# Interleaving each block's product with rounded weights and its product with the weights' rest on TensorE

## The chip, the cores and the metric

The kernel runs on one core of one Trainium2 chip. The time is device microseconds of one execution. All times in the tables are medians of several executions of the same program.

## What is computed

Two transformer blocks are applied to one sequence of 256 tokens with 1024 features, everything in 32-bit floats. Cut to the matrix products that matter here, the reference is:

```python
# first block
x = x + 0.5 * swiglu(rms_norm(x, ffn1_norm), w_gate, w_up, w_down)      # gu0, down0
u = rms_norm(x, mix_norm) @ w_in                                        # w_in
x = x + concat([fourier_mixer(u), gqa_attention(u)]) @ w_out            # w_out
x = x + 0.5 * swiglu(rms_norm(x, ffn2_norm), w_gate, w_up, w_down)      # gu1, down1
x = rms_norm(x, final_norm)
# second block, layers 0 and 1
x = x + short_conv_mixer(h, conv_w_in, conv_w, conv_w_out)              # conv_in, conv_out
x = x + moba_attention(h, ...)                                          # moba, moba_o
x = x + mem_cross_attention(h, mem, w_q, w_kv, w_o)                     # mem0, mem_o0; mem1, mem_o1
x = x + (silu(g) * u) @ w_down      # g, u = split(h @ w_gu)            # gu2, down2; gu3, down3
```

The names behind the `#` are the phases of the kernel.

## The kernel before

**How a product is made.** TensorE multiplies 32-bit numbers fast only in a rounded form (fp32r). So each weight matrix W and each operand A is split in two rounded parts, W = Wh + Wl and A = Ah + Al, and three of the four products are added up: Wh Ah, Wh Al and Wl Ah. Ah and Al of the 256 tokens lie side by side in SBUF, so one matmul with Wh (helper `with_hi`, L418) streams 512 columns and writes Wh Ah into columns 0 to 255 of a PSUM bank and Wh Al into columns 256 to 511. A second matmul with Wl (L462 in square tiles, `with_rest`, L422, in the down phases) streams the 256 columns of Ah and adds to columns 256 to 511 of the same bank. Here these are called the 512-column and the 256-column products. Each has a 128x128 weight load of its own.

**Tiles.** All weights form one stream of 205 tiles (list `STREAM`) of 16 blocks of 128x128. Tile t lies in slot t % 3. SyncE loads it (L354; L365 to L369 for the down phases), ScalarE rounds it (L916, semaphore `weight_hi`), VectorE subtracts to get the rest (L1271, semaphore `weight_lo`), and TensorE uses both. TensorE counts `tile_done` behind its last product; on that ScalarE overwrites the slot's rounded half with tile t+3 and copies the second column half of the result out of PSUM (`rest`, L928). VectorE adds the two halves (L1376), scales them (L1400), makes the next tile's rest but one (L1271) and finishes the nonlinear part (L1416, L1422).

**Order on TensorE.** A square tile (`square_tile`, L424; 8 row blocks k by 2 output blocks m) waits for `weight_hi`, runs its 16 products of 512 columns, waits for `weight_lo`, runs its 16 products of 256 columns. First tiles of a phase are cut into shorter pieces (`cuts`), since their operand arrives in pairs of row blocks. Tiles that share TensorE with attention come in pieces (`PIECES`, `ks`). `value_tile` (L493) does the same with the roles of weights and operand swapped, with both weight parts needed from the start. `down` (L604) runs 16 blocks of a tile in the same two runs in `run` (L612). The phases `w_in` and `moba` use another form (`narrow`), where all products have 256 columns.

The engines' own programs set the order; there is no scheduler. The queue of each engine runs in order and waits at semaphores.

Of the kernel before, what the change touches and what calls it, by code (L numbers as in the profile page):

```python
# [14 lines left out]
S = 256  # L15
D = 1024
KB = D // P
KP = KB // 2
NT = S // P
# [30 lines left out]
for _name, _n in STREAM:  # L50
# [22 lines left out]
    ("mem1", [B, C, A, B] + [A, B] * 3), ("mem_o1", [A, B, C, A]),  # L73
    ("gu3", [B, C, A] * 7 + [B]), ("down3", [C, A, DD, B]),
]


NARROW = ("w_in", "moba")
# [96 lines left out]
def program(nc, weights, x_t, mem_t, vectors, consts, fourier, fnet_w, positions, out_t):  # L175
    ctx = ExitStack()
    with ctx:
# [237 lines left out]
        def _(pe):  # L415
# [8 lines left out]
            def square_tile(t, out, a, ready=None, beside={}, lows=None, ks=(0, KB), ms=2, cuts=(), narrow=False, late=None):  # L424


                w = wt[t % RING]
                for k0, k1 in zip((ks[0], *cuts), (*cuts, ks[1])):
# [24 lines left out]
                    if rest_first:  # L453
                        continue
                    if lows is not None:
                        pe.wait_ge(*lows(k0))
                    elif k0 == 0:
                        pe.wait_ge(weight_lo, t + 1)
                    for k in range(k0, k1):
                        for m in range(ms):  # L460
                            home = out[:, m, 0:S] if narrow else out[:, m, S:2 * S]
                            mm = pe.matmul(home, w[:, 1, m * KB + k, :], a[:, k, 0, :], start=False, stop=k == KB - 1,  # L462
                                           skip_group_check=True)
                if late is not None and narrow:
# [28 lines left out]
            def value_tile(t, out, a, beside={}, ks=(0, KB), narrow=False):  # L493

                w = wt[t % RING][:].rearrange("p a (m k) c -> p a m k c", m=2)
                if narrow:
                    narrow_values(t, out, a, w, beside, ks)
                    return
                o = [out[:, n, :].rearrange("p (a m c) -> p a m c", a=2, m=2) for n in range(NT)]
                tok = [slice(n * P, (n + 1) * P) for n in range(NT)]  # L500
                if ks[0] == 0:
                    pe.wait_ge(weight_lo, t + 1)
                for k in range(*ks):
                    if k in beside:
# [79 lines left out]
            def gate_up(n, name):  # L584
# [3 lines left out]
                for j in range(FF):  # L588
                    ready = operand(name) if j == 0 else None
                    in_parts = n == 0 and j < RING  # L590
                    lows = None
                    if in_parts and j == 0:
                        ready = lambda k: ([(first_split, 1)] if k == 0 else [(split_done, 1)] if k == 1 else operand(name)(k)) + (
                            [] if k % 2 else [(first_hi, 1)] if k == 0 else [(start_hi, k // 2)] if k < KB - 2 else [(weight_hi, 1)])
                        lows = lambda k: (start_lo, k // 2 + 1) if k < KB - 2 else (weight_lo, 1)
                    elif in_parts:
                        ready = lambda k: {0: [(start_hi, KP - 2 + j)], KB // 2: [(weight_hi, j + 1)]}.get(k, [])
                        lows = lambda k: (weight_lo, j + 1) if k else (start_lo, KP - 1 + j)
                    square_tile(t0 + j, banks_for(phase, j), xn, ready=ready, lows=lows,
                                beside={**norm(name, n == 0).get(j, {}), **tables.get(j, {})}, ms=1 if j == FF - 1 and n < 2 else 2,  # L600
                                cuts=((2, 4, 6) if j == 0 else (4,)) if in_parts else (4, 6) if j == 0 else (),
                                late=KP * OPERAND[name] if j == 0 and n else None)

            def down(n_ffn, norm_name, beside={}):  # L604
# [4 lines left out]

                    return [(8 * half0 + 4 * n, k) for n, k in enumerate(ks)]  # L610

                def run(i, rows, d, ms, fresh=False, final=None):  # L612

                    w = wt[(t0 + i) % RING]
                    blocks = [(at + m, k, m, bank[:, 2 * PAIR[name, 2 * d + m // 2] + m % 2, :])
                              for at, k in rows for m in ms]
                    for at, k, m, out in blocks:
                        if k == FF - 1 and name in SHORT:
                            pe.matmul(out[:, 0:S], w[:, 0, at, :], h[:, k, 0, :], start=False, stop=False, skip_group_check=True)
                        else:  # L620
                            with_hi(out, w[:, 0, at, :], h[:, k], k == 0)
                    if fresh:
                        pe.wait_ge(weight_lo, t0 + i + 1)
                    for at, k, m, out in blocks:
                        mm = with_rest(out, w[:, 1, at, :], h[:, k], k == final)
                        if k == final and (d, m) in ((0, 1), (0, 3), (1, 1), (1, 2)):
                            mm.then_inc(acc_done, 1)
                    return mm

                def final_run(i):  # L630
# [17 lines left out]
                for i in range(FF // 2):  # L648
# [5 lines left out]
                    if i <= FF // 4:  # L654
                        pe.wait_ge(h_split, FF * n_ffn + min(4 * i + 4, FF))
                    if i < FF // 4:
                        mm = run(i, rows_at(0, range(4 * i, 4 * i + 4)), 0, range(4), True)
# [19 lines left out]
            def residual(name, ready, b0=0, b1=KP, ks=None):  # L677

                for b in range(b0, b1):
                    k0, k1 = ks or (BEGUN.get(name, {}).get(b, 0), KB)  # L680
                    square_tile(FIRST[name] + b, banks_for(name, b, k0 == 0), h, ready=ready if b < 2 else None, ks=(k0, k1),
                                cuts=(6,) if b == 0 and k0 < 6 < k1 else ())

            def part(kind, j, ks=(0, KB), **more):
                what = PARTS[kind][j][0]
# [5 lines left out]
                if what == "v":  # L691
                    value_tile(t, out, src, ks=ks, beside=more.get("beside", {}), narrow=kind in NARROW)
                else:
                    square_tile(t, out, src, ks=ks, narrow=kind in NARROW, **more)

            def pieces(kind, n, i, ready):
                for j, k0, k1 in PIECES[kind][n][i]:
# [174 lines left out]
            for j in range(COUNT["conv_in"]):  # L872
                square_tile(FIRST["conv_in"] + j, banks_for("conv_in", j), xn, ready=operand("mix0") if j == 0 else None,
                            cuts=() if j else (4, 6), late=None if j else KP * OPERAND["mix0"],
                            beside={1: {5: both_sums}, 2: {1: lambda: spread_factor("mix0")}, 3: {1: lambda: spread_column(col_1, SPREAD_AT["mix0 first"], 0)}}.get(j, {}))
            for ks in ((0, 6), (6, KB)):
                for b in range(2):
# [1118 lines left out]
```

## Time and profile before

| | before |
|---|---|
| median of 3 executions | 1240.01 us |
| lowest, highest | 1239.48, 1240.45 us |
| span of the profiled execution, first to last instruction | 1237.7 us |
| TensorE busy | 1229.1 us (99%) |
| TensorE weight loads busy | 1095.2 us (88%) |
| VectorE busy | 928.1 us (75%) |
| ScalarE busy | 658.7 us (53%) |
| bytes moved | 221.74 MB |

The profiled execution is shown by its span; the median of the timed ones lies 2.3 us above it. Matmuls overlap in the profile (a product's recorded time includes its way through the array), so how fast they follow each other is read from the starts of rows, not from the duration of one. In a row of the timeline the first number is the start and the second the time from the start of the first to the end of the last instruction of a merged group; `PE` are matmuls and `PEld` the weight loads.

### The profile page before, as it was taken

Reading aid. Unit: us, or ns where it says so; the run is one execution under the profiler, and the core shown is the slowest. Engines: PE = TensorE matmul, PEld = TensorE weight load, DVE = VectorE, ACT = ScalarE, POOL = GpSimd, SP = SyncE. Lnnn points to the kernel's source line nnn. Section 1 sums busy time; section 2 is a strip of 40 time slices with the busy share of each in tenths; the row PEclk is TensorE's granted clock in tenths of the full one; section 3 lists DMA queues with packets and bytes.
Section 4 is the critical chain, followed back from the end, with each engine's and each line's share of the span. In section 5 each row is a group of like instructions: output and inputs, shape, how many; then the busy total and the mean of one; then the engine's idle time right before and its main releaser. Section 6 shows DMA issues by size and latency. Waiting matters only on the chain.

```text
span 1237.7 us, 18082 instructions
## 1 busy us (share of the span) xinstructions
PE 1229.1 (99%) x7432; PEld 1095.2 (88%) x7432; DVE 928.1 (75%) x1292; ACT 658.7 (53%) x872; POOL 31.1 (3%) x23
## 2 busy tenths in 40 slices
PE   9999999999999999999999999999999999999998
PEld 8888889978888888888888888889998888888887
DVE  7887866878777858988568777669968657877744
ACT  6655544456555444546546555445555445555632
POOL 0000000000000000440000000000000000000000
PEclk9999999999999999999999999999999999999999
DMA  9565664235555663556346555644445533555560
GB/s 329 187 213 177 224 209 164 75 137 172 187 186 188 214 216 131 186 188 211 130 138 233 188 190 186 222 170 152 156 142 182 187 136 137 204 200 177 198 209 34
DMA packets 51426, 221.74 MB, mean 179 GB/s; under 512 B 4464, under 2 KB 5776, under 8 KB 30864
## 3 DMA queue, kind: packets, MB, share of 16 engines
q1 hardware_dynamic: 51056, 220.25, 51.7%
q8 instruction: 59, 0.97, 0.3%
q10 hardware_dynamic: 288, 0.33, 0.1%
q14 instruction: 23, 0.19, 0.0%
HBM read 219.52 MB, written 1.05 MB: 178 GB/s over the span
## 4 chain that ended last, share of the span: by engine, by line
PE 92%; DVE 5%; issue 1%; DMA 1%; ACT 0%; SPq 0%; DVEq 0%; ACTq 0%
PE bank L418 48%; PE bank L462 21%; PE bank L422 7%; PE bank L449 5%; PE bank L507 2%; DVE wt L1271 2%; PE bank L761 2%; PE bank L789 2%; PE bank L484 1%; PE bank L510 1%; PE bank L489 1%; DMA raw<-weights 1%; PE bank L777 0%; PE bank L544 0%; DVE xn L1280 0%
## 5 line engine op out<-in xcount | busy, mean ns | idle before, releaser
L1271 DVE TENSOR_TENSOR wt<-raw,wt 128x2048 fp32r<-128x2048 f32 x202 | 464.1, 2299 | 67.8 <-ACT wt L916 67.4
L916 ACT ACTIVATE wt<-raw 128x2048 fp32r<-128x2048 f32 x202 | 386.0, 1911 | 119.7 <-PE bank L422 89.8
L418 PE MATMUL bank<-xn,wt 128*128 128x512 f32 x1712 | 416.3, 393 | 1.4 <-DVE scratch L1376 0.7
L418 PEld LDWEIGHTS bank<-xn,wt 128*128 128x128 f32 x1712 | 313.0, 188 | 63.0 <-DVE xn L1280 1.1
L418 PE MATMUL bank<-h,wt 128*128 128x512 f32 x1004 | 246.1, 392 | 0.0
L462 PEld LDWEIGHTS bank<-xn,wt 128*128 128x128 f32 x1824 | 234.3, 191 | 9.7 <-DVE wt L1271 0.8
L462 PE MATMUL bank<-xn,wt 128*128 128x256 f32 x1824 | 238.2, 283 | 0.2 <-DVE wt L1271 0.2
L418 PEld LDWEIGHTS bank<-h,wt 128*128 128x128 f32 x1004 | 182.5, 188 | 34.1 <-issue 0.4
L1376 DVE TENSOR_TENSOR scratch<-bank,rest 128x512 f32<-128x512 f32 x98 | 67.6, 690 | 86.9 <-ACT rest L928 86.8
L999 ACT ACTIVATE h<-scratch 128x256 fp32r<-128x256 f32 x88 | 36.8, 418 | 158.7 <-DVE scratch L1416 158.7
L928 ACT ACTIVATE rest<-bank 128x512 f32<-128x512 f32 x114 | 67.6, 593 | 65.9 <-PE bank L462 64.4
L422 PEld LDWEIGHTS bank<-h,wt 128*128 128x128 f32 x700 | 91.8, 191 | 4.6
L422 PE MATMUL bank<-h,wt 128*128 128x256 f32 x700 | 93.5, 282 | 0.0
L1400 DVE TENSOR_TENSOR scratch<-scratch,r_x 128x512 f32<-128x512 f32 x86 | 59.5, 692 | 2.9
L955 ACT ACTIVATE xn<-x,vec 128x256 fp32r<-128x256 f32 x62 | 28.1, 501 | 55.6 <-DVE x L1286 55.6
L462 PEld LDWEIGHTS bank<-h,wt 128*128 128x128 f32 x384 | 50.9, 191 | 2.8
L462 PE MATMUL bank<-h,wt 128*128 128x256 f32 x384 | 52.0, 282 | 0.0
L1285 DVE SCALAR_TENSOR_TENSOR x<-bank,x 128x512 f32<-128x512 f32 (+1 forms) x39 | 24.9, 637 | 30.6 <-PE bank L462 18.1
L1416 DVE TENSOR_TENSOR scratch<-scratch 128x256 f32<-128x256 f32 x88 | 36.7, 417 | 4.7 <-ACT scratch L997 4.7
L997 ACT ACTIVATE scratch<-scratch 128x256 f32<-128x256 f32 x88 | 35.7, 406 | 6.0 <-DVE scratch L1400 5.0
L449 PE MATMUL bank<-xn,wt 128*128 128x256 f32 x280 | 38.1, 288 | 0.0
L1422 DVE TENSOR_TENSOR h<-scratch,h 128x256 fp32r<-128x256 f32 x88 | 36.7, 417 | 0.6 <-ACT h L999 0.2
(227 smaller groups left out, 972.3 us busy)
## 6 DMA issues: line engine op xcount, KB each, us to landing
raw<-weights SPq DMA_DIRECT2D x158, 1024.0 KB, 4.9
raw<-weights SPq DMA_DIRECT2D x88, 512.0 KB, 4.9
raw<-weights SPq DMA_DIRECT2D x8, 256.0 KB, 4.5
k_t<-mem_t SPq DMA_DIRECT2D x2, 1024.0 KB, 8.1
raw<-weights SPq DMA_DIRECT2D x8, 128.0 KB, 4.1
out_t<-work SPq DMA_DIRECT2D x4, 256.0 KB, 2.3
x<-x_t SPq DMA_DIRECT2D x3, 256.0 KB, 5.3
v_s<-fourier SPq DMA_DIRECT2D x2, 256.0 KB, 5.3
```

The lines of the kernel that those rows point to most:

```text
L418: return pe.matmul(out, hi, a.rearrange("p a s -> p (a s)"), start=first, stop=False, skip_group_check=True)
L422: return pe.matmul(out[:, S:2 * S], lo, a[:, 0, :], start=False, stop=last, skip_group_check=True)
L449: pe.matmul(out[:, m, 0:S], w[:, 0, m * KB + k, :], a[:, k, i, :], start=k == i == 0, stop=False, skip_group_check=True)
L462: mm = pe.matmul(home, w[:, 1, m * KB + k, :], a[:, k, 0, :], start=False, stop=k == KB - 1, skip_group_check=True)
L916: act.activation(wt[t % RING][:, 0], raw[t % RING][:], ACT.Copy).then_inc(weight_hi, 1)
L928: act.activation(rest_s[i % 3][:], src, ACT.Copy).then_inc(rest_copied, 1)
L999: act.activation(h[:, j, 0, :], gate, ACT.Copy).then_inc(h_rounded, 1)
L1271: dve.tensor_tensor(wt[t % RING][:, 1], raw[t % RING][:], wt[t % RING][:, 0].bitcast(F32), ALU.subtract).then_inc(weight_lo, 1)
L1376: e = dve.tensor_tensor(dst, pair_banks(name, j)[:, :, 0:S], rest_s[i % 3][:], ALU.add)
L1400: dve.tensor_tensor(gu_s[j % 3], gu_s[j % 3], both(r_x[:]), ALU.mult).then_inc(drained, 1)
L1416: dve.tensor_tensor(gate, gate, up, ALU.mult).then_inc(whole, 1)
L1422: dve.tensor_tensor(h[rows, j, i, :], gu_s[j % 3][rows, 0, :], h[rows, j, 0, :].bitcast(F32), ALU.subtract).then_inc(h_split, 1)
```

## The change

Each 256-column product is issued right behind the 512-column product of a block, for the same block or for one that lies `lag` row blocks back. With lag 0 the two alternate strictly: 512, 256, 512, 256. With lag L a tile starts with 2L products of 512 columns, goes on in alternation, and ends with 2L products of 256 columns (beside the last pair's own). A table `LAG` gives the lag by phase and tile; other whole tiles have 0, and tiles that begin as a piece have 2. The wait for `weight_lo` moves from behind all 512-column products of a tile to behind the first 2L. In `run` of `down` the lag counts blocks, and only the tiles 0 and 1 of each down phase have one (10 blocks). `value_tile` alternates its two kinds as well (two and two). What stays as it was: the first tiles of phases with `cuts`, the narrow phases, the last products of the program (`final_run`), all counts of instructions, and the programs of the other four engines.

```diff
+LAG = {**{(f"gu{n}", j): (4 if n == 0 else {1: 5}.get(j, 3)) for n in range(4) for j in range(14 if n == 0 else 7)},
+       **{(f"down{n}", i): 5 for n in range(4) for i in range(2)},
+       **{("conv_in", j): 8 if j < 6 else 6 if j < 9 else 4 for j in range(12)},
+       ("w_out", 2): 8, ("w_out", 3): 5, ("conv_out", 0): 4, ("conv_out", 1): 4, ("conv_out", 2): 6, ("conv_out", 3): 4,
+       ("mem_o0", 2): 6, ("mem_o0", 3): 4, ("mem_o1", 2): 6, ("mem_o1", 3): 4,
+       **{("moba_o", b): 2 for b in range(4)},
+       ("mem0", 1): 7, ("mem0", 2): 3, ("mem1", 1): 5, ("mem1", 2): 2}
+
+def lag_of(name, j, k0, k1):
+    return min(LAG.get((name, j), 2 if k1 < KB else 0), k1 - k0) if k0 == 0 else 0
...
                 w = wt[t % RING]
+                if lag is not None:
+                    if ks[0] == 0:
+                        pe.wait_ge(weight_hi, t + 1)
+                    for k in range(ks[0], ks[1] + lag):
...
+                        if ks[0] == 0 and k == lag:
+                            pe.wait_ge(weight_lo, t + 1)
+                        for m in range(ms):
+                            if k < ks[1]:
+                                with_hi(out[:, m, :], w[:, 0, m * KB + k, :], a[:, k], k == 0)
+                            if k - lag >= ks[0]:
+                                mm = with_rest(out[:, m, :], w[:, 1, m * KB + k - lag, :], a[:, k - lag], k - lag == KB - 1)
+                    if ks[1] == KB:
+                        mm.then_inc(tile_done, 1)
+                    return
...
-                for k in range(*ks):
-                    for n in range(NT):
                         mm = pe.matmul(o[n][:, 1], a[:, k, 1, tok[n]], w[:, 0, :, k, :], start=False, stop=k == KB - 1,
...
-                    if fresh:
-                        pe.wait_ge(weight_lo, t0 + i + 1)
-                    for at, k, m, out in blocks:
-                        mm = with_rest(out, w[:, 1, at, :], h[:, k], k == final)
...
+                    for n in range(len(blocks) + lag):
+                        if n < len(blocks):
+                            at, k, m, out = blocks[n]
...
+                                with_hi(out, w[:, 0, at, :], h[:, k], k == 0)
+                        if n == lag and fresh:
+                            pe.wait_ge(weight_lo, t0 + i + 1)
+                        if n >= lag:
+                            at, k, m, out = blocks[n - lag]
+                            mm = with_rest(out, w[:, 1, at, :], h[:, k], k == final)
```

TensorE's order in phase gu3, tiles 11 and 12 (slots wt0 and wt1), in the kernel before:

```order
L418 MATMUL bank<-xn,wt0 128x512 [waits weight_hi,taken]
L418 MATMUL bank<-xn,wt0 128x512 x15
L462 MATMUL bank<-xn,wt0 128x256 [waits weight_lo]
L462 MATMUL bank<-xn,wt0 128x256 x15
L418 MATMUL bank<-xn,wt1 128x512 [waits weight_hi,taken]
```

The same place after the change, from the end of tile 11 into tile 12 (lag 0):

```order
L431 MATMUL bank<-xn,wt0 128x512
L435 MATMUL bank<-xn,wt0 128x256
L431 MATMUL bank<-xn,wt1 128x512 [waits weight_lo,weight_hi,taken]
L435 MATMUL bank<-xn,wt1 128x256
L431 MATMUL bank<-xn,wt1 128x512
L435 MATMUL bank<-xn,wt1 128x256
L431 MATMUL bank<-xn,wt1 128x512
L435 MATMUL bank<-xn,wt1 128x256
```

L431 and L435 are `with_hi` and `with_rest` in the changed file. The wait for the rest of the weights has moved from the seventeenth product of a tile to its first.

TensorE's order in phase gu0, tile 4 (slot wt1), in the kernel before:

```order
L418 MATMUL bank<-xn,wt1 128x512 [waits weight_hi,taken]
L418 MATMUL bank<-xn,wt1 128x512 x15
L462 MATMUL bank<-xn,wt1 128x256 [waits weight_lo]
L462 MATMUL bank<-xn,wt1 128x256 x15
```

And after, where the lag of this tile and its neighbours is 4 (what follows the rows shown is more of the same alternation, and then nine products of 256 columns in a row):

```order
L431 MATMUL bank<-xn,wt1 128x512 [waits weight_hi,taken]
L431 MATMUL bank<-xn,wt1 128x512 x7
L431 MATMUL bank<-xn,wt1 128x512 [waits weight_lo]
L435 MATMUL bank<-xn,wt1 128x256
L431 MATMUL bank<-xn,wt1 128x512
L435 MATMUL bank<-xn,wt1 128x256
```

The wait for the rest has moved from behind 16 products to behind 8. In the whole program a 256-column product follows a 512-column one directly at 240 places before and at 2,223 after, and 2,120 single 256-column products stand behind a single 512-column one, where before there was none. All of it is on TensorE; the order of the other engines' instructions is the same.

## Rows read from the trace of the kernel before

**Rows 1.** The page: span, busy time by engine, granted clock, chain by engine.

```profile
span 1237.7 us, 18082 instructions
...
PE 1229.1 (99%) x7432; PEld 1095.2 (88%) x7432; DVE 928.1 (75%) x1292; ACT 658.7 (53%) x872; POOL 31.1 (3%) x23
...
PEclk9999999999999999999999999999999999999999
...
PE 92%; DVE 5%; issue 1%; DMA 1%; ACT 0%; SPq 0%; DVEq 0%; ACTq 0%
```

**Rows 2.** The waits of TensorE: for whom, us in total, times, longest.

```profile
PE bank L418 <- DVE scratch L1376: 0.7, 1, 0.7
...
PE bank L462 <- DVE wt L1271: 0.2, 1, 0.2
```

**Rows 3.** Timeline of TensorE in gu3: start, us, engine, line, operation, count.

```profile
1100.12 3.82 PE L418 MATMUL bank<-xn,wt 128*128 128x512 f32 x16
1103.77 2.08 PE L462 MATMUL bank<-xn,wt 128*128 128x256 f32 x16
1105.68 3.82 PE L418 MATMUL bank<-xn,wt 128*128 128x512 f32 x16
1109.34 2.08 PE L462 MATMUL bank<-xn,wt 128*128 128x256 f32 x16
1111.25 3.82 PE L418 MATMUL bank<-xn,wt 128*128 128x512 f32 x16
```

**Rows 4.** The timeline cut narrowly, to see each run's second product start.

```profile
1105.92 0.40 PE L418 MATMUL bank<-xn,wt 128*128 128x512 f32 x1
...
1103.88 0.40 PE L462 MATMUL bank<-xn,wt 128*128 128x256 f32 x2
```

**Rows 5.** Timeline of TensorE in w_out, where runs are two long.

```profile
279.74 0.63 PE L418 MATMUL bank<-h,wt 128*128 128x512 f32 x2
280.21 0.39 PE L462 MATMUL bank<-h,wt 128*128 128x256 f32 x2
280.44 0.63 PE L418 MATMUL bank<-h,wt 128*128 128x512 f32 x2
280.90 0.40 PE L462 MATMUL bank<-h,wt 128*128 128x256 f32 x2
281.13 0.63 PE L418 MATMUL bank<-h,wt 128*128 128x512 f32 x2
```

**Rows 6.** Timeline of TensorE at the end of down0: runs of three, one bank each.

```profile
189.60 0.86 PE L418 MATMUL bank<-h,wt 128*128 128x512 f32 x3
190.30 0.52 PE L422 MATMUL bank<-h,wt 128*128 128x256 f32 x3
190.66 0.86 PE L418 MATMUL bank<-h,wt 128*128 128x512 f32 x3
191.35 0.52 PE L422 MATMUL bank<-h,wt 128*128 128x256 f32 x3
191.71 3.71 PE L449 MATMUL bank<-xn,wt 128*128 128x256 f32 x28
```

**Rows 7.** Timeline of VectorE in gu3: the chain that ends with a weight rest.

```profile
1106.51 0.69 DVE L1376 TENSOR_TENSOR scratch<-bank,rest 128x512 f32<-128x512 f32 x1 [1.28 <-ACT rest L928]
1107.24 0.69 DVE L1400 TENSOR_TENSOR scratch<-scratch,r_x 128x512 f32<-128x512 f32 x1
1107.85 2.28 DVE L1271 TENSOR_TENSOR wt<-raw,wt 128x2048 fp32r<-128x2048 f32 x1
```

**Rows 8.** Timeline in gu0, tiles 5 and 6: TensorE's starts and VectorE's rests.

```profile
36.97 3.82 PE L418 MATMUL bank<-xn,wt 128*128 128x512 f32 x16
37.00 2.29 DVE L1271 TENSOR_TENSOR wt<-raw,wt 128x2048 fp32r<-128x2048 f32 x1
...
42.45 2.28 DVE L1271 TENSOR_TENSOR wt<-raw,wt 128x2048 fp32r<-128x2048 f32 x1
...
42.54 3.82 PE L418 MATMUL bank<-xn,wt 128*128 128x512 f32 x16
```

**Rows 9.** Timeline in conv_in, tiles 9 and 11: VectorE's rests, TensorE's starts.

```profile
525.47 2.28 DVE L1271 TENSOR_TENSOR wt<-raw,wt 128x2048 fp32r<-128x2048 f32 x1
...
525.97 3.82 PE L418 MATMUL bank<-xn,wt 128*128 128x512 f32 x16
...
536.75 2.27 DVE L1271 TENSOR_TENSOR wt<-raw,wt 128x2048 fp32r<-128x2048 f32 x1
...
537.10 3.82 PE L418 MATMUL bank<-xn,wt 128*128 128x512 f32 x16
```

More of the change, by code:

```diff
@@ L422, in with_rest, with square_tile @@
                 return pe.matmul(out[:, S:2 * S], lo, a[:, 0, :], start=False, stop=last, skip_group_check=True)
-            def square_tile(t, out, a, ready=None, beside={}, lows=None, ks=(0, KB), ms=2, cuts=(), narrow=False, late=None):
+            def square_tile(t, out, a, ready=None, beside={}, lows=None, ks=(0, KB), ms=2, cuts=(), narrow=False, late=None, lag=None):
                 w = wt[t % RING]
+                if lag is not None:
+                    if ks[0] == 0:
+                        pe.wait_ge(weight_hi, t + 1)
+                    for k in range(ks[0], ks[1] + lag):
+                        if k < ks[1] and ready is not None:
+                            for s, value in ready(k):
+                                pe.wait_ge(s, value)
+                        if k < ks[1] and k in beside:
+                            beside[k]()
+                        if ks[0] == 0 and k == lag:
[8 more added lines that the diff above has]
+                    return
                 for k0, k1 in zip((ks[0], *cuts), (*cuts, ks[1])):
@@ L601, in gate_up @@
                                 cuts=((2, 4, 6) if j == 0 else (4,)) if in_parts else (4, 6) if j == 0 else (),
+                                lag=None if in_parts or j == 0 else lag_of(phase, j, 0, KB),
                                 late=KP * OPERAND[name] if j == 0 and n else None)
@@ L610, in rows_at, with run @@
                     return [(8 * half0 + 4 * n, k) for n, k in enumerate(ks)]
-                def run(i, rows, d, ms, fresh=False, final=None):
+                def run(i, rows, d, ms, fresh=False, final=None, lag=0):
                     w = wt[(t0 + i) % RING]
@@ L616, in run @@
                               for at, k in rows for m in ms]
-                    for at, k, m, out in blocks:
[L618 to L621, printed above, removed]
-                    if fresh:
-                        pe.wait_ge(weight_lo, t0 + i + 1)
-                    for at, k, m, out in blocks:
-                        mm = with_rest(out, w[:, 1, at, :], h[:, k], k == final)
-                        if k == final and (d, m) in ((0, 1), (0, 3), (1, 1), (1, 2)):
-                            mm.then_inc(acc_done, 1)
+                    for n in range(len(blocks) + lag):
+                        if n < len(blocks):
+                            at, k, m, out = blocks[n]
+                            if k == FF - 1 and name in SHORT:
+                                pe.matmul(out[:, 0:S], w[:, 0, at, :], h[:, k, 0, :], start=False, stop=False, skip_group_check=True)
+                            else:
+                                with_hi(out, w[:, 0, at, :], h[:, k], k == 0)
[4 more added lines that the diff above has]
+                            mm = with_rest(out, w[:, 1, at, :], h[:, k], k == final)
+                            if k == final and (d, m) in ((0, 1), (0, 3), (1, 1), (1, 2)):
+                                mm.then_inc(acc_done, 1)
                     return mm
@@ L656, in down @@
                     if i < FF // 4:
-                        mm = run(i, rows_at(0, range(4 * i, 4 * i + 4)), 0, range(4), True)
+                        mm = run(i, rows_at(0, range(4 * i, 4 * i + 4)), 0, range(4), True, lag=2 * LAG.get((name, i), 0))
                     elif i == FF // 4:
@@ L681, in residual @@
                     square_tile(FIRST[name] + b, banks_for(name, b, k0 == 0), h, ready=ready if b < 2 else None, ks=(k0, k1),
-                                cuts=(6,) if b == 0 and k0 < 6 < k1 else ())
+                                cuts=(6,) if b == 0 and k0 < 6 < k1 else (),
+                                lag=None if b == 0 and k0 < 6 < k1 else lag_of(name, b, k0, k1))
             def part(kind, j, ks=(0, KB), **more):
@@ L693, in part @@
                 else:
-                    square_tile(t, out, src, ks=ks, narrow=kind in NARROW, **more)
+                    square_tile(t, out, src, ks=ks, narrow=kind in NARROW,
+                                lag=None if kind in NARROW else lag_of(kind, j, *ks), **more)
             def pieces(kind, n, i, ready):
@@ L874, in _ @@
                             cuts=() if j else (4, 6), late=None if j else KP * OPERAND["mix0"],
+                            lag=lag_of("conv_in", j, 0, KB) if j else None,
                             beside={1: {5: both_sums}, 2: {1: lambda: spread_factor("mix0")}, 3: {1: lambda: spread_column(col_1, SPREAD_AT["mix0 first"], 0)}}.get(j, {}))
```

## The prediction

> **What bounds the kernel now.** I read the page first: TensorE is busy for 1229.1 of 1237.7 us, the chain that ended last runs over TensorE for 92% of the span, and the granted clock stands at nine tenths or more of full speed, the level of 2.4 GHz, in all 40 slices [rows 1]. Then the list of waits: the longest that TensorE stood still for another engine is 0.7 us, and for a weight rest it waited once, 0.2 us [rows 2]. So no wait is left whose removal could pay. What remains is how fast products follow each other. That is read from starts in the timeline, not from durations, because matmuls overlap. In gu3 the starts of three 512-column runs are 1100.12, 1105.68 and 1111.25 [rows 3]: two tiles of 16 + 16 products in 11.13 us, or 11.13 / 32 = 0.3478 us for one pair of a 512- and a 256-column product. Inside, 16 products of 512 take 1103.77 - 1100.12 = 3.65 us and 16 of 256 take 1105.68 - 1103.77 = 1.91 us, so 228 and 119 ns each. The column counts alone, at 2.4 GHz, are 213 and 107 ns, so each product, long or short, carries some 13 to 15 ns beyond its columns. That is the whole stake of this change: it takes away no product and no weight load, it only changes which product follows which.
>
> **The change, part by part: the pace.** The instruction order shows 2,120 single 256-column products that come to stand directly behind a single 512-column one. The price of such a pair in strict alternation is nowhere in this trace: the shortest runs are two long. It must be bounded from rows.
>
> Runs of two: the starts 279.74, 280.44 and 281.13 [rows 5] give 1.39 us for four pairs, 0.3475 us a pair. Runs of three, three products into one PSUM bank each: 189.60 to 191.71 [rows 6] is 2.11 us for six pairs, 0.3517 us. Runs of sixteen: 0.3478 us [rows 3]. The upper bound is that of the runs of three. It is not monotone: the blocks of three are dearer than both of the others, and those of two are as cheap as those of sixteen.
>
> The lower bound comes from the edges of long runs. The first 256-column product behind a 512-column run lasts 1103.88 - 1103.77 = 0.11 us to the next start [rows 3, 4], less than the 0.119 of its run. The first 512-column product behind a 256-column run lasts 1105.92 - 1105.68 = 0.24 us [rows 3, 4], while the other fifteen of a run have (3.65 - 0.24) / 15 = 0.227. If alternation kept the cheap edge and paid nothing for it, a pair would cost 0.11 + 0.227 = 0.337 us. If it paid both edges, 0.11 + 0.24 = 0.35 us. I take the runs of two, since they are the nearest thing to alternation that the trace has: 0.3475. Against the present 0.3478 that is 2,120 x -0.3 ns = -0.6 us. The ends of the range are 2,120 x -10.8 ns = -22.9 us and 2,120 x +3.9 ns = +8.3 us.
>
> That a 256-column product adds to the very bank that the product before it writes should cost nothing: in the runs of three with one bank each the step from the last 512 to the first 256 is part of 190.30 - 189.60 = 0.70 us for three [rows 6], 0.23 each, no gap among them. That holds for the lagged tiles too, since block m of both kinds goes to the same bank.
>
> A rule of the Trainium skill speaks against a gain here. Its page "TensorE: Matmul & The Clock Gate" (section "Step-by-step: what each phase is for") says that the next weights are loaded while the running matmul streams, and (section "LDWEIGHTS (loading the stationary operand)") that a load of 128 columns takes about 107 ns. By that each short product just covers the load of the next and each long one covers it twice over, and alternation leaves the number of loads under short products as it was, so its sum would be no change in pace. Its figures for the gap (section "Back-to-back issue gap": 518 and 262 cycles, 216 and 109 ns) would give 325 ns a pair in either order; the trace has 348, so the measured number stands.
>
> **The change, part by part: the wait for the weights' rest.** Before, 16 products of 512 columns (3.65 us) covered VectorE's subtraction at the start of a tile. Now 2L of them do, and none at lag 0. What stands behind the waiting instruction is the whole rest of the tile on TensorE, and behind that `tile_done`, for which ScalarE's copy and next rounding wait. So lateness would go into the end of the tile one to one. I compare for each kind of tile the end of the rest with the moment of the new wait.
>
> Steady tiles of gu1, gu2, gu3 (lag 0): the chain behind a finished tile is L1376, L1400, L1271, and ends at 1107.85 + 2.28 = 1110.13 [rows 7]; the tile that needs it starts at 1111.25 [rows 3]. It is 1.12 us early with no cover at all: free. It hangs on the end of a TensorE tile, so it moves with it, and would still be free with tiles shorter by a tenth.
>
> Gu0, tiles 5 to 9 (lag 4): tile 5 starts at 36.97 and its rest is ready at 37.00 + 2.29 = 39.29. The old wait came at 36.97 + 3.65 = 40.62, the new one after eight products at 36.97 + 8 x 0.228 = 38.79: late by 0.50 us. Tile 6 starts at 42.54, and with the shift of 0.50 its wait comes at 44.86, behind the rest at 42.45 + 2.28 = 44.73 [rows 8]. So this is paid once.
>
> Conv_in, where VectorE is busiest: tile 9 would wait at 525.97 + 1.82 = 527.79, its rest is there at 527.75; tile 11 at 537.10 + 1.82 = 538.92 with the rest at 539.02, late by 0.10 us [rows 9]. Each late wait also costs the weight load that can't be issued ahead, about one short interval of 0.11 us [rows 4]. Sum: 0.50 + 0.10 + 2 x 0.11 = +0.8 us. It is bounded below by 0 (the engines before it may shift a little, too) and above by about 3 us, if some six tiles of this kind lose 0.5 each as the one in gu0.
>
> Nothing else moves: all other queues (SyncE's loads wait for `weight_lo`, which VectorE gives at the same place of its program) have the same order, and the products at the end of the program keep theirs. Earlier `acc_done` marks in the down phases feed VectorE, which isn't on the path.
>
> **Sum.** -0.6 + 0.8 = +0.2 us. The profiled span of 1237.7 us lies 2.3 us below the median of the timed runs; I add the change to the median: 1240.0 + 0.2 = 1240.2 us.
>
> **The rivals.**
>
> A, faster: the short product's extra time belongs to a run of short ones, where one weight load treads on the heels of the next. Then alternation keeps the cheap edge of 0.11 us at all 2,120 places. For it: the first short product of each run is faster than the others [rows 3, 4]. Against it: the first long product behind a short run is slower by about as much (0.24 against 0.227), and runs of two show no gain. Full price: -22.9 + 0.8, 1217.9 us. Half of it: 1229.4 us.
>
> B, slower: changing from short to long costs the long ones something, as the dearer runs of three show. The number of such changes goes from 207 to 2,188 in the instruction order. Price at the pace of runs of three: +8.3 + 0.8, 1249.1 us. It decides from a pair of 0.3486 us on, where 2,120 x 0.8 ns + 0.8 us make 2.5 us. Against it: the runs of two.
>
> C, slower by waits: more tiles of gu0 and conv_in come late to their rests. Up to +3 us, 1243 us; it lies at the edge of what can be told from no change. If A holds, these waits grow, since VectorE there doesn't get faster.
>
> **How the numbers follow.** A measurement of this kernel can tell about 0.2%, 2.5 us, from no change. The forecast's own case, a pair between 0.3465 and 0.3486 us, gets 0.46. A gets 0.30: two thirds of it for up to half of its price, one third for more. B gets 0.20 and C 0.04. So faster by over 0.2%: 0.30; within 0.2%: 0.46; slower: 0.24. The range goes from 1228 us (half of A and a little more) to 1249 us (all of B but its tail); what is left out is the far part of A and the tail of B.
>
> **What would show it.** In the profile after, the distance of two tile starts in gu3 divided by 16 is the pair: 0.3475 us if I am right, 0.34 or less for A, 0.35 or more for B. The waits of TensorE should name L1271 with about 1 us in all, most of it near 38.8 us in gu0, and next to nothing in gu3. The weight loads should still be 7,432, and the granted clock unchanged. I am wrong in the main if the distance of gu3 tiles leaves 5.55 to 5.58 us, since 2,120 pairs multiply each nanosecond of it into 2.1 us.

## The result, and the profile after

The changed kernel takes 1249.09 us (four runs, 1248.88 to 1249.15), the kernel before 1239.93 us on the same chip (four runs, 1239.48 to 1240.45). The ratio is 1.0074, with a 95% interval of 1.0062 to 1.0086: slower by 9.2 us. The forecast said 1240.2 and no difference. The profiled executions show the same step: the span goes from 1237.7 us [rows 1] to 1247.3 us.

The page of the changed kernel: span, busy time by engine (share, instructions), the granted clock, and the chain that ended last, by engine.

```profile
span 1247.3 us, 18090 instructions
...
PE 1238.6 (99%) x7432; PEld 1092.5 (88%) x7432; DVE 928.7 (74%) x1292; ACT 659.4 (53%) x872; POOL 31.1 (2%) x23
...
PEclk9999999999999999999999999999999999999999
...
PE 91%; DVE 6%; ACT 1%; issue 1%; DMA 1%; SPq 0%; DVEq 0%; ACTq 0%
```

TensorE has the same 7,432 products and 7,432 weight loads as in [rows 1], the same clock, and 9.5 us more busy time. VectorE and ScalarE did the same work in the same time. So the kernel did not begin to wait for another engine; the products themselves follow each other more slowly. The waits of TensorE for what the change could touch (for whom, us in total, times, longest) confirm it:

```profile
PE bank L431 <- DVE scratch L1413: 0.8, 1, 0.8
...
PE bank L431 <- DVE wt L1308: 0.3, 1, 0.3
PE bank L435 <- DVE wt L1308: 0.2, 1, 0.2
```

The first is the wait that [rows 2] had too (0.7). The second is new and is the late weight rest of gu0; the third was there before. Together they explain well under 1 us of the 9.6. (`with_hi` is at line 431 now, `with_rest` at 435, the weight rest at 1308.)

The rest is in the distance of tiles. VectorE makes one weight rest per tile right behind the tile before, so its starts are a clean ruler. Three rests in gu3 of the changed kernel (start, duration):

```profile
1110.09 2.28 DVE L1308 TENSOR_TENSOR wt<-raw,wt 128x2048 fp32r<-128x2048 f32 x1
...
1115.74 2.29 DVE L1308 TENSOR_TENSOR wt<-raw,wt 128x2048 fp32r<-128x2048 f32 x1
...
1121.40 2.29 DVE L1308 TENSOR_TENSOR wt<-raw,wt 128x2048 fp32r<-128x2048 f32 x1
```

Two tiles in 11.31 us, where [rows 3] had 11.13. A pair now takes 11.31 / 32 = 0.3534 us, not 0.3478. But this is not the pace everywhere. The start times in two cuts of TensorE's timeline, the first from gu3 and the second from the late tiles of gu0, which run the very same order of instructions (one 512-column product, one 256-column product, lag 0):

```profile
1107.92 0.40 PE L431 MATMUL bank<-xn,wt 128*128 128x512 f32 x1
1108.15 0.28 PE L435 MATMUL bank<-xn,wt 128*128 128x256 f32 x1
1108.27 0.40 PE L431 MATMUL bank<-xn,wt 128*128 128x512 f32 x1
...
1108.63 0.40 PE L431 MATMUL bank<-xn,wt 128*128 128x512 f32 x1
...
1108.98 0.40 PE L431 MATMUL bank<-xn,wt 128*128 128x512 f32 x1
...
1110.04 0.40 PE L431 MATMUL bank<-xn,wt 128*128 128x512 f32 x1
```

```profile
120.06 0.39 PE L431 MATMUL bank<-xn,wt 128*128 128x512 f32 x1
...
120.41 0.39 PE L431 MATMUL bank<-xn,wt 128*128 128x512 f32 x1
...
120.76 0.39 PE L431 MATMUL bank<-xn,wt 128*128 128x512 f32 x1
...
122.14 0.39 PE L431 MATMUL bank<-xn,wt 128*128 128x512 f32 x1
```

In gu3 six pairs take 1110.04 - 1107.92 = 2.12 us, 0.3533 a pair, and the steps go 0.35, 0.36, 0.35: one pair in three is longer. In gu0 six pairs take 122.14 - 120.06 = 2.08 us, 0.3467 a pair, with even steps. I call these the **slow pace** and the **fast pace**. The same order of products has two prices, 6.7 ns apart, and each lasts for many tiles: all of gu1, gu2 and gu3 from tile 7 on run slow, the late tiles of gu0 run fast. Both can stand in one phase: in down1 the 52 pairs from 428.20 us on run slow, then come nine 256-column products in a row, and the 72 pairs from 447.53 us on run fast. Of all pairs in stretches of 20 or more, 1,160 ran slow and 216 fast. Both levels are above 0.320 us, which is 768 columns at 2.4 GHz, so the fast pace is 13.3 ns beyond the columns for each product, just what the long products in runs of sixteen have (0.227 us). Split by product (starts in the trace to the nanosecond, means over the 240 pairs of gu3), the slow pace is 236.7 ns for the long and 116.7 for the short one. The fast pace, in the late tiles of gu0, is 230.0 and 116.7. So in both the short product is cheaper than the 120 ns that it has within a run, and in both the long one is dearer than its 227; the two paces differ in the long product alone.

By phase, each counted from its first product to that of the next phase, changed kernel minus kernel before: gu0 +1.2, down0 +0.8, gu1 +1.5, down1 +0.3, gu2 +1.6, down2 +0.8, gu3 +1.5, down3 +0.8, the other ten phases together +1.4; sum +9.9. The span grew by 9.6, because the first product of gu0 starts 0.3 us earlier in this trace; 0.24 of gu0's 1.2 is that start and not the change. In gu3, 15 tiles at 5.653 us in place of 5.567 make 1.3 of the 1.5; the lagged tiles before them make the rest. Down1 lost less than the other down phases, since most of its strict pairs ran fast.

One thing said of the change above is not so in the code: `value_tile` alternates one by one, like the other tiles, and not two and two. In the diff both products stand in the same inner loop, and in mem0 the trace has 512, 256, 512, 256 columns from 569.11 us on.

### The profile page after: what moved, and what is told of

It is laid out like the page before. It is cut to its first block, busy times and chain, and to the rows that moved or that the text cites. A ratio compares the mean times of both kernels' runs of the same rounds, so it can differ in the third digit from the quotient of the medians.

```text
span 1247.3 us, 18090 instructions
## 1 busy us (share of the span) xinstructions
PE 1238.6 (99%) x7432; PEld 1092.5 (88%) x7432; DVE 928.7 (74%) x1292; ACT 659.4 (53%) x872; POOL 31.1 (2%) x23
## 4 chain that ended last, share of the span: by engine, by line
PE 91%; DVE 6%; ACT 1%; issue 1%; DMA 1%; SPq 0%; DVEq 0%; ACTq 0%
PE bank L431 48%; PE bank L435 24%; PE bank L481 5%; PE bank L494 3%; PE bank L539 2%; DVE wt L1308 2%; PE bank L825 2%; PE bank L797 2%; PE bank L516 1%; PE bank L540 1%; PE bank L521 1%; DMA raw<-weights 1%; PE bank L813 0%; PE bank L574 0%; DVE scratch L1413 0%
## 5 line engine op out<-in xcount | busy, mean ns | idle before, releaser
L431 PE MATMUL bank<-xn,wt 128*128 128x512 f32 x1712 | 553.6, 398 | 1.6 <-DVE scratch L1413 0.8
L435 PE MATMUL bank<-xn,wt 128*128 128x256 f32 x1632 | 392.8, 281 | 0.2 <-DVE wt L1308 0.2
L431 PEld LDWEIGHTS bank<-xn,wt 128*128 128x128 f32 x1712 | 317.1, 188 | 74.6 <-DVE wt L1308 1.1
L431 PE MATMUL bank<-h,wt 128*128 128x512 f32 x1004 | 328.9, 397 | 0.0
L435 PEld LDWEIGHTS bank<-xn,wt 128*128 128x128 f32 x1632 | 283.2, 189 | 5.4 <-DVE wt L1308 0.8
L435 PE MATMUL bank<-h,wt 128*128 128x256 f32 x1012 | 247.9, 281 | 0.0
L431 PEld LDWEIGHTS bank<-h,wt 128*128 128x128 f32 x1004 | 186.7, 188 | 42.7 <-issue 0.4
L435 PEld LDWEIGHTS bank<-h,wt 128*128 128x128 f32 x1012 | 177.8, 189 | 2.4
L539 PE MATMUL bank<-wt,mn 128*128 128x512 f32 x128 | 46.1, 402 | 0.0
L481 PE MATMUL bank<-xn,wt 128*128 128x256 f32 x280 | 38.1, 288 | 0.0
L540 PE MATMUL bank<-wt,mn 128*128 128x256 f32 x128 | 35.9, 280 | 0.0
```

The source lines that it names most:

```text
L431: return pe.matmul(out, hi, a.rearrange("p a s -> p (a s)"), start=first, stop=False, skip_group_check=True)
```

## The experiments

**First question: what sets the pace?** In front of the stretch in gu0 that is fast, the last lagged tile has lag 4; in front of those that are slow in gu1 to gu3 it has lag 3. A lag of L row blocks leaves 2L long products ahead, so 16 - 2L pairs, and then 2L short products behind. Theory (P in the expectations): the pace is a cycle that TensorE falls into, and where the tile before it is cut decides which. The rivals: the phase decides, by its other work (S: traffic of VectorE, ScalarE and the transfers), or every change between long and short has its price (C, the prediction's rival B).

**e1_residue**: the changed kernel with one more row block of lag in tile 6 of gu1 to gu3, and half a row block more in tile 1 of the down phases.

```
-LAG = {**{(f"gu{n}", j): (4 if n == 0 else {1: 5}.get(j, 3)) ...
-       **{(f"down{n}", i): 5 for n in range(4) for i in range(2)},
+LAG = {**{(f"gu{n}", j): (4 if n == 0 else {1: 5, 6: 4}.get(j, 3)) ...
+       **{(f"down{n}", i): (5, 5.5)[i] for n in range(4) for i in range(2)},
```

> The changed kernel with two numbers of the table of lags altered: tile 6 of gu1, gu2 and gu3 has lag 4 in place of 3 (8 alternating pairs in it, not 10), and tile 1 of each down phase 11 blocks in place of 10 (5 pairs, not 6). Theory P (phase): strict alternation has two paces, 0.3533 us a pair (three pairs in 1.06 us) and 0.3467 us (three in 1.04 us), and which of them a stretch gets is set by where the stretch before was cut: 2, 5, 8 or 11 pairs behind a long run of 512-column products lead to the fast one. Then tiles 7 to 21 of gu1 to gu3 take 5.547 us each, not 5.653, the down tiles behind tile 1 likewise: 45 x -0.106 - some 25 x -0.1, together about -7 us, 1242 us. Theory C (each change from 256 to 512 columns costs the long product something, whatever came before): the number of changes is the same but for 9, so 1249 us. Theory S (the place decides: other engines' traffic in SBUF and PSUM): gu1 to gu3 keep 5.653, 1249 us.

Measured: 1244.11 us (1244.03 to 1244.52), ratio to before 1.0034 (1.0021 to 1.0047), 5.0 us below the changed kernel. Its weight rests in gu3:

```profile
1095.39 2.28 DVE L1308 TENSOR_TENSOR wt<-raw,wt 128x2048 fp32r<-128x2048 f32 x1
1100.94 2.29 DVE L1308 TENSOR_TENSOR wt<-raw,wt 128x2048 fp32r<-128x2048 f32 x1
...
1123.12 2.28 DVE L1308 TENSOR_TENSOR wt<-raw,wt 128x2048 fp32r<-128x2048 f32 x1
```

Five tiles in 27.73 us, 5.546 each: fast. Tiles 7 to 21 have not one instruction in another order than in the changed kernel; only tile 6 in front of them differs, and the 232 pairs (gu1) or 240 pairs (gu2, gu3) behind it changed pace. The three phases lost their 1.5 or 1.6 us each and stand 0.02 to 0.09 below the kernel before. So the price isn't that of the alternation itself, nor of the place in the kernel. The down phases stayed as they were, against the expectation: that half of the rule was wrong.

**e2_lags**: the same tile 6 with lag 7 in gu1, 5 in gu2 and 6 in gu3.

```
-LAG = {**{(f"gu{n}", j): (4 if n == 0 else {1: 5}.get(j, 3)) ...
+LAG = {**{(f"gu{n}", j): (4 if n == 0 else {1: 5, 6: {1: 7, 2: 5, 3: 6}[n]}.get(j, 3)) ...
```

> The changed kernel with the lag of tile 6 set apart by phase: 7 in gu1 (2 alternating pairs), 5 in gu2 (6 pairs), 6 in gu3 (4 pairs). Theory P: only gu1 gets the fast pace behind it (remainder 2 by 3), tiles of 5.547 us; gu2 and gu3 keep 5.653. A rival within P, that a longer lag as such or a later wait gives the fast pace: all three are fast. Theories C and S: none is. Time: 1249.1 - 15 x 0.106 = 1247.5 us by P, 1244.3 by the rival, 1249.1 by C and S.

Measured, one run: 1249.14 us, all three phases slow (1.4 to 1.5 us above the kernel before, each); the one expected to be fast (gu1, lag 7) was slow as well. So a rule by the number of pairs alone is not enough. Read product by product (starts to the nanosecond), the short products behind the cut have a rhythm of their own, whose longest step is 124 ns against 117 to 121 for the others. In the tiles that led to the fast pace, the run of short ones was left behind that long step: it was 9 long there, and 15 in gu1 here. From this the next runs' rule: of runs behind eight pairs, those of 9 and of 14 short products (the last pair's own counted) give the fast pace, the others the slow one.

**Second question: does it hold without the rest of the change?** **e3_strict** is the kernel before, in its two separate runs everywhere, but with tiles 7 to 21 of gu1 to gu3 in strict alternation. **e4_strict_kick** is e3 with tile 6 at lag 4 in front of them.

```
 e3:  LAG = {(f"gu{n}", j): 0 for n in (1, 2, 3) for j in range(7, FF)}
 e4:  LAG = {(f"gu{n}", j): 4 if j == 6 else 0 for n in (1, 2, 3) for j in range(6, FF)}
 both (a tile not in the table keeps its two runs):
      return min(LAG.get((name, j), KB), k1 - k0)
```

> The kernel before (two runs in each tile) with one part of the change: tiles 7 to 21 of gu1, gu2 and gu3 alternate strictly (lag 0), all else in two runs as before. Theory P: entered from a long run of 256-column products the stretch is slow, 5.653 us a tile against 5.567, 45 x 0.086 = +3.9 us over the kernel before, 1243.8 us. Theory C: the same, +3.9 us. My forecast on record would have been a pair of 0.3475 us and no difference.

> As the run before it, and tile 6 of the three phases has lag 4 (8 alternating pairs in front of the strict stretch). Theory P: the fast pace, 5.547 us a tile against 5.567 of two runs: 45 x -0.020 + 3 x 0.038 = -0.8 us against the kernel before, 1239.2 us, and 4.7 us below the run before it. Theories C and S: 45 x 0.086 + 3 x 0.04, +4.0 us, 1243.9 us, the same as the run before it.

Measured: e3 1243.55 us (1243.15 to 1244.74), ratio 1.0032 (1.0021 to 1.0044); e4 1239.16 us (1238.90 to 1239.97), ratio 0.9997 (0.9988 to 1.0006). This is the cleanest pair of the study: one number in the table moves the time by 4.4 us. TensorE's timeline at the beginning of the alternation in gu3, first e3 and then e4 (start, duration, line, operation, count):

```profile
1080.22 3.82 PE L425 MATMUL bank<-xn,wt 128*128 128x512 f32 x16
1083.88 2.08 PE L429 MATMUL bank<-xn,wt 128*128 128x256 f32 x16
...
1086.14 0.40 PE L425 MATMUL bank<-xn,wt 128*128 128x512 f32 x1
...
1086.50 0.40 PE L425 MATMUL bank<-xn,wt 128*128 128x512 f32 x1
...
1088.26 0.40 PE L425 MATMUL bank<-xn,wt 128*128 128x512 f32 x1
```

```profile
1078.32 2.23 PE L425 MATMUL bank<-xn,wt 128*128 128x512 f32 x9
...
1082.85 1.25 PE L429 MATMUL bank<-xn,wt 128*128 128x256 f32 x9
1083.93 0.40 PE L425 MATMUL bank<-xn,wt 128*128 128x512 f32 x1
...
1084.63 0.39 PE L425 MATMUL bank<-xn,wt 128*128 128x512 f32 x1
...
1086.71 0.39 PE L425 MATMUL bank<-xn,wt 128*128 128x512 f32 x1
```

Six pairs take 1088.26 - 1086.14 = 2.12 us in e3 and 1086.71 - 1084.63 = 2.08 us in e4: 353.3 and 346.7 ns. In e3 each of the three phases is 1.3 us longer than before, in e4 0.2 to 0.3 us shorter. The first two pairs of e4's stretch take 351 and 352 ns; from the third on the fast pace is there, and it stays to the end of the phase. Both forecasts of theory P were met within 0.3 us.

**Third question: is it the surroundings?** **e5_quiet** is the kernel before with 13 stretches of products behind its end, when every other engine and all transfers are idle. The stretches are long runs, some pairs, short runs of different lengths, and then 24 or 48 strict pairs; some put the short products into other banks than the long ones.

```
 for _ in range(longs):  long_one()
 for _ in range(pairs):  long_one(); short_one()
 for _ in range(shorts): short_one()
 for _ in range(strict): long_one(); short_one(other)
```

> The kernel before, and behind its end, when all other engines and the DMA are done, 13 stretches of strict alternation on TensorE alone, each behind 16 long products (512 columns) that level out what came before, then n alternating pairs, then a run of short products (256 columns), then 48 or 24 strict pairs; and 12 times two long, two short. The time is longer by these stretches, some 200 us, and tells nothing. Theory P, which the traces so far make sharper: the fast pace of 0.3467 us a pair needs n = 2 by remainder 3 and a run of short ones of 9 (8 and the last of the pairs) or 14, for that run then has a rhythm of five (121, 120, 124, 118, 117 ns) and has to end behind the 124. So: n = 0, 16 short ones: slow, 0.3533; n = 8 with 8 more: fast; the same two where the strict short products go to other banks than the long ones: unchanged, slow and fast; straight behind the long run: slow; n = 6 and n = 7: slow; n = 8 with 9, 10, 11, 12, 14 more: slow, with 13 more: fast. Theory S (traffic of other engines): with all others idle there is one pace only, 0.3467, in every stretch. Theory B (a short product that adds to the bank just written pays): other banks give 0.3467 where the same bank gave 0.3533. Two and two: 0.348 to 0.349 us a pair.

Measured: all 13 stretches ran at the pace that was expected of them. A window of this part (busy time of each engine, with instructions; granted clock, DMA share, GB/s), and then the cuts of the timeline in which two of the stretches begin and end:

```profile
1300.00:1350.00 50.00, 50.00 (x284) 43.59 (x283) 0.00 (x0) 0.00 (x0) 0.00 (x0) 1.00 0.00 1
```

```profile
1260.70 0.40 PE L418 MATMUL bank<-xn,wt 128*128 128x512 f32 x1
...
1277.66 4.04 PE L418 MATMUL bank<-xn,wt 128*128 128x512 f32 x17
1284.00 1.25 PE L422 MATMUL bank<-xn,wt 128*128 128x256 f32 x9
1285.09 0.40 PE L418 MATMUL bank<-xn,wt 128*128 128x512 f32 x1
...
1301.73 3.83 PE L418 MATMUL bank<-xn,wt 128*128 128x512 f32 x16
```

Behind 16 long and 16 short products, 48 pairs take 1277.66 - 1260.70 = 16.96 us, 353.3 ns each. Behind eight pairs and 9 short products, 48 pairs take 1301.73 - 1285.09 = 16.64 us, 346.7 ns each. With nothing else running on the core the two paces are the same as inside the kernel, as closely as these cuts can be read (0.2 ns a pair), so traffic and contention aren't what makes them two. With the short products in other banks the means were 353.4 and 346.9: the bank has no part either. Behind eight pairs, short runs of 10, 11, 12, 13 and 15 gave 352.7 to 353.3, and the run of 14 gave 347.1:

```profile
1470.95 1.85 PE L422 MATMUL bank<-xn,wt 128*128 128x256 f32 x14
...
1472.64 0.40 PE L418 MATMUL bank<-xn,wt 128*128 128x512 f32 x1
...
1480.97 4.06 PE L418 MATMUL bank<-xn,wt 128*128 128x512 f32 x17
```

(24 pairs in 8.33 us). Behind six or seven pairs a run of 9 gave 353.4 and 353.3. The end of this part held runs of two, as those of [rows 5]: 348.3 ns a pair.

**Fourth question: the late weight rest.** **e6_wait** is the changed kernel with lag 8, that is two separate runs, in tile 5 of gu0.

```
-... (4 if n == 0 else {1: 5}.get(j, 3)) ...
+... ((8 if j == 5 else 4) if n == 0 else {1: 5}.get(j, 3)) ...
```

> The changed kernel with tile 5 of gu0 in two runs (lag 8): its wait for the weights' rest stands behind 16 products again. In the trace of the changed kernel the start of tile 6 lies 0.60 us further behind the kernel before than the start of tile 5. If that is the late rest, it falls to about 0.0 and tile 7 pays at most 0.1; the phase of later stretches is not touched, since tiles 6 to 13 keep their lag: about -0.5 us in all, 1248.6 us. If it is pace, it stays.

Measured, one run: 1248.91 us. First the wait in the changed kernel, then the same place in e6, one tile later:

```profile
37.13 1.99 PE L431 MATMUL bank<-xn,wt 128*128 128x512 f32 x8
39.42 0.50 PE L431 MATMUL bank<-xn,wt 128*128 128x512 f32 x1 [0.30 <-DVE wt L1308]
39.76 0.28 PE L435 MATMUL bank<-xn,wt 128*128 128x256 f32 x1
```

```profile
37.29 3.81 PE L431 MATMUL bank<-xn,wt 128*128 128x512 f32 x16
40.94 2.08 PE L435 MATMUL bank<-xn,wt 128*128 128x256 f32 x16
42.85 2.62 PE L431 MATMUL bank<-xn,wt 128*128 128x512 f32 x9
45.31 0.28 PE L435 MATMUL bank<-xn,wt 128*128 128x256 f32 x1
```

In the changed kernel the eight long products would end at 37.13 + 8 x 0.228 = 38.95; the next starts at 39.42, 0.47 us late, and the step to its short product is 0.34 in place of 0.23 us. That is 0.58 us, and the tile is 0.60 us longer than before. In e6 it is gone there, but the next tile's nine long products and their gap take 45.31 - 42.85 = 2.46 us, where the same nine in the changed kernel's later tiles take 2.06: the wait was moved on by a tile and cost 0.40 us there, against the expectation of at most 0.1. VectorE is behind TensorE at that point of gu0, and in both kernels the first tile with half of the cover paid for it. The time, 0.2 us below the changed kernel's, fits the two numbers but couldn't show them by itself.

**Last: does the fast pace beat the kernel before?** **e7_fast** keeps the two separate runs, and in gu0 to gu3 and the down phases places one tile with eight pairs and then strict alternation.

```
 KICK = (13, 6, 6, 6)
 LAG = {(f"gu{n}", j): 4 if j == KICK[n] else 0 for n in range(4) for j in range(KICK[n], FF)}
 ... (down phases) lag=(16, 8, 0, 0, 0)[i]
```

> The kernel before with strict alternation only where the rest of the weights is early without cover, and each such stretch entered at the fast pace: tile 13 of gu0, tile 6 of gu1 to gu3 and tile 1 of each down phase have lag 4 (8 pairs, run of 9 short ones), the tiles behind them to the end of the phase lag 0; everything else in two runs. Theory P: gu0 8 tiles, gu1 to gu3 45 tiles and the down phases some 32, each 5.547 in place of 5.567 us, and 8 entry tiles at +0.04: 85 x -0.020 + 8 x 0.04 = -1.4 us, 1238.3 us. Theory C: 85 x 0.086 + 0.3, +7.6 us, 1247 us.

Measured: 1239.49 us (1238.99 to 1240.57, 11 runs) against 1239.80 (14 runs), ratio 0.9998 (0.9989 to 1.0008): no difference that can be told, 1.2 us above the expectation. By the trace six of its eight stretches were fast and gained 0.06 to 0.27 us each; down0 and the first part of down1 ran slow and lost 0.67 and 0.24. In down0 the tile with the eight pairs itself ran otherwise than in the later phases:

```profile
136.08 0.50 PE L571 MATMUL bank<-weigh,work 128*128 128x1 f32 x4
136.44 2.33 PE L426 MATMUL bank<-h,wt 128*128 128x512 f32 x9
138.61 0.28 PE L430 MATMUL bank<-h,wt 128*128 128x256 f32 x1
...
139.42 0.39 PE L426 MATMUL bank<-h,wt 128*128 128x512 f32 x1
...
140.11 0.39 PE L426 MATMUL bank<-h,wt 128*128 128x512 f32 x1
```

Four products of one column stand just ahead of it, and its pairs then ran in steps of 0.35 and 0.34 us, 0.69 us for two, where in the later phases they have the steps of the slow pace. The nine short products behind them don't end with a step of 124 ns, and the pace that followed was slow. That the one-column products are the cause isn't shown. Down1 speaks against them as the whole of it: no one-column product stands ahead of its tile, yet its eight pairs (from 421.36 us on) ran at the fast pace, and behind the same nine short ones the 52 pairs were slow. So the number of pairs and of short products doesn't settle the pace by itself; the steps in which the pairs run differ too, and what sets those is open.

## Why the prediction was wrong

**The step that failed is the price of a pair.** The working took 0.3475 us from the runs of two [rows 5] as the nearest thing to alternation, and made 2,120 x -0.3 ns = -0.6 us of it. The runs measured 0.3533 us in most stretches and 0.3467 us in a few. Over the whole kernel the phases show 9.9 us more; less 0.2 for the earlier start and 0.7 for the late rests (0.6 in gu0, 0.1 in conv_in) this is 9.0 / 2,120 = 4.2 ns a pair over the old 0.3478, so 0.3520 on average. The term was -0.6 and is +9.0. The forecast's own sign of being wrong was a distance of gu3 tiles outside 5.55 to 5.58 us; it is 5.653. Single stretches lie even above the upper bound of 0.3517 that I took from the runs of three [rows 6], and the fast ones are far above the lower bound of 0.337.

**What was wrong behind it** is the assumption that strict alternation has one price, for which short runs are a nearer and nearer stand-in. It has two, 2% apart, and TensorE stays in the one it enters. The rows hinted at this: blocks of three were dearer than both those of two and those of sixteen, which I wrote down as "not monotone" and then resolved by nearness. A price that isn't monotone in the length of the runs can't be carried to length one by nearness; it called for the wide chance on the slower side. The working also held the better term and passed it over: "if it paid both edges, 0.11 + 0.24 = 0.35 us". By it the term is 2,120 x +2.2 ns = +4.7 us. The slow pace pays about both edges: a short product of 0.117 us and a long one of 0.237.

**Rival A's premise fell.** The short product does keep a part of its cheap edge in alternation, 0.117 us in the mean against 0.120 in a run, but never without a dearer long one, 0.230 or 0.237 against 0.227. The cheap pair of 340 ns comes once, as the first of a lagged tile behind long products; the second has 350 already. In the fast pace a pair costs the columns and 13.3 ns for each product, as the long products in long runs do. What the short runs of the kernel before lose against that is 1.2 ns a pair. So at the best steady pace that any run showed there were 2,120 x 1.2 ns = 2.5 us to win, about what a measurement can just tell, and at the slow one 2,120 x 5.5 ns = 11.7 us to lose.

**Rival B had the time, and half of the mechanism.** It forecast 1249.1 us by a price that the long product pays for each change from short to long. A long product behind a short one does take longer, by 10 ns at the slow pace and by 3 at the fast one. But that is no fixed price: e1 has as many such changes as the changed kernel but for some ten in 2,188, e4 has some twenty more than e3, and they take 5.0 and 4.4 us less. That the sum agrees to the tenth of a microsecond is luck. B took 0.3517 us, close to the mean of 0.3520, from two pairs of blocks of three, read to 0.01 us [rows 6]. All four such pairs of blocks at the end of down0 in the kernel before, from 187.50 to 191.71 us, give 4.21 / 12 = 0.3508, and B would have said 1247.2.

**The waits were right.** The list of waits named the weight rest in gu0, at the tile and within 0.1 us of the size forecast (0.60 against 0.50 + 0.11). The steady tiles of gu1 to gu3 wait for nothing, as the chain of [rows 7] said. "Paid once" was right too; e6 shows that it is paid once even when the tile is spared. Conv_in is +0.3 us in all. Of it the late rests make 0.1, half of the forecast: the first pair takes 0.42 us in tile 8 (526.94 us) and 0.36 in tile 11, in place of 0.34. Rival C's 3 us didn't come.

**A rule weighed in the prediction.** The sum from the loads of weights was no change in pace, since the number of loads under short products is kept. The runs at hand decide otherwise: the pace changed by -1.2 or +5.5 ns a pair with the same loads. The Trainium skill's page "TensorE: Matmul & The Clock Gate" (section "Step-by-step: what each phase is for") has the next weights loaded under the running matmul. The trace agrees: in the changed kernel loads are busy for 1092.5 us and products for 1238.6 of the same 1247.3. But it doesn't tell the pace to a percent.

**What stays open** is what inside TensorE makes the two cycles. Shown by e5 to have no part in there being two: other engines, transfers, the bank, waits and the clock (1.00 for both); the number of products and loads is the same too. A wait or another product in between can still decide which of the two follows. That it is the phase between loading weights and streaming columns is a guess; no run here tells it from another one. The rule by the length of the last short run (9 or 14 behind eight pairs) foretold all 13 stretches of e5, but it missed where the tile before was entered otherwise (down0 and down1 in e7). In the changed kernel nine short products in a row stand ahead of 72 pairs in both down0 and down1, and the pairs are slow in the first and fast in the second. So the rule describes this order and is no law.

## What to carry to other kernels

When TensorE is the bound and a change only reorders its products, price the new order in its steady state, and don't infer it from short runs of another shape: here six pairs in one cycle take 2.12 us and in another 2.08 us, and 2,000 of them make 13 us. Read the distance of tiles in each phase after such a change, since the same code can run at two paces; if it does, try the cut of the tile in front before giving the order up. And compute first what a perfect order could win (columns plus the fixed part seen in the best rows): here that was 2.5 us of 1240, a fifth of what the slow pace can cost.

## What the runs showed that was not expected

Products of 512 and 256 columns in strict alternation, each with its own weight load, run at 353.3 or 346.7 ns a pair at the same granted clock of 1.00, and keep that pace over 240 pairs when nothing comes in between. The slow pace is a cycle of three pairs, 1.06 us; the fast one is 1.04 us for three. The quiet stretches of e5 repeat both, within 0.2 ns a pair.

Which one is taken can be set from outside: eight pairs and then nine short products, in place of ten pairs and seven short ones, in a single tile ahead, moved the 232 to 240 pairs behind it to the fast pace in each of three phases (e1).

The cut alone doesn't settle it. In e7 the same eight pairs and nine short products led to the fast pace in six stretches and to the slow one in down0 and down1, where the eight pairs had themselves run in other steps. Four one-column products stand ahead of the tile in down0, none in down1; no run tries them by themselves.
